# SwiGLU products of the prompt rows by one level of Strassen's scheme, with f and sums of w_down kept in DRAM between the gate/up and the down products

## The reference

```python
h = rmsnorm(x, g_pre_ffn)          # (1024 + 64, 1024)
gu = h @ w_gu                      # w_gu (1024, 2 * 2816)
gate, up = gu[..., :D_FF], gu[..., D_FF:]
f = (jax.nn.silu(gate) * up) @ w_down   # w_down (2816, 1024)
x = x + rmsnorm(f, g_post_ffn)
```

## Time and profile before

| | us |
|---|---|
| median of 3 runs (lowest, highest) | 1645.95 (1645.14, 1646.17) |
| span of the profiled execution | 1641.7 |
| around the span, to the median | 4.25 |
| PE busy | 1556.9 (95%) |
| DVE, ACT, POOL busy | 614.3, 410.7, 384.7 |
| output projection starts | about 721 |
| feed-forward part, from the first unit's matmul to the end | about 833 to 1641.7 |

### The profile page before, as it was taken

How to read it: one execution, slowest core, us unless ns; L and a number is a source line. 1 busy time by engine, 2 the same in 40 slices (tenths; PEclk the granted TensorE clock), 3 DMA queues, 4 the chain that set the end, 5 groups by cost and what they waited for, 6 DMA issues and landing times.

```text
span 1641.7 us, 23152 instructions
## 1 busy us (share of the span) xinstructions
PE 1556.9 (95%) x9350; PEld 1343.4 (82%) x9350; DVE 614.3 (37%) x983; ACT 410.7 (25%) x730; POOL 384.7 (23%) x459
## 2 busy tenths in 40 slices
PE   7999999998888889989999999999999999999994
PEld 6788888878655557768899999999999999999983
DVE  2334110106866545424532233332323333332355
ACT  4301121212254434433332121111112111111121
POOL 3254300013422212004462121211212121111111
PEclk9999999999999999999999999999999999999997
DMA  6323434129354029934356354544535354453434
GB/s 216 112 81 128 128 128 164 48 76 318 111 197 136 14 118 419 409 123 135 101 164 187 121 154 113 154 134 140 160 108 161 110 156 138 131 161 108 133 119 168
DMA packets 120290, 245.59 MB, mean 150 GB/s; under 512 B 20652, under 2 KB 82364, under 8 KB 115045
## 3 DMA queue, kind: packets, MB, share of 16 engines
q1 hardware_dynamic: 111400, 157.15, 29.8%
q0 software_dynamic: 6976, 71.32, 14.1%
q10 hardware_dynamic: 1824, 15.83, 2.3%
HBM read 214.08 MB, written 106.21 MB: 195 GB/s over the span
## 4 chain that ended last, share of the span: by engine, by line
PE 48%; POOL 3%; issue 2%; DVE 2%; ACT 0%; POOLq 0%; ACTq 0%; DVEq 0%
PE y_ps L2198 32%; PE x_ps L2212 8%; PE m_ps L2212 4%; PE d_ps L2212 4%; POOL xm L1671 1%; POOL h_lo L1683 1%; PE y_ps L1801 1%; DVE y L1766 1%; DVE acc L2129 0%; DVE acc L2133 0%; POOL stat L1664 0%; POOL stat L1673 0%; POOL stat L2008 0%; DVE acc L2117 0%; DVE m_lo L1740 0%
## 5 line engine op out<-in xcount | busy, mean ns | idle before, releaser
L2198 PE MATMUL y_ps<-h_hi,gu_hi 128*128 128x384 f32 (+1 forms) x1056 | 345.9, 328 | 0.0
L2198 PE MATMUL y_ps<-h_hi,gu_lo 128*128 128x384 f32 (+1 forms) x1056 | 345.5, 327 | 0.0
L2198 PE MATMUL y_ps<-h_lo,gu_hi 128*128 128x384 f32 (+1 forms) x1056 | 345.5, 327 | 0.0
L1976 POOL TENSOR_TENSOR f<-silu,f 128x384 fp32r<-128x384 f32 (+1 forms) x66 | 60.4, 915 | 605.0 <-ACT f L2038 417.8
L2198 PEld LDWEIGHTS y_ps<-h_lo,gu_hi 128*128 128x128 f32 x1056 | 198.3, 188 | 2.0
L2198 PEld LDWEIGHTS y_ps<-h_hi,gu_hi 128*128 128x128 f32 x1056 | 198.2, 188 | 2.0
L2198 PEld LDWEIGHTS y_ps<-h_hi,gu_lo 128*128 128x128 f32 x1056 | 198.2, 188 | 0.0
L514 PE MATMUL z_ps<-w_hi,h_hi 128*128 128x512 f32 x488 | 191.2, 392 | 4.3 <-POOL h_lo L342 4.3
L514 PE MATMUL z_ps<-w_lo,h_hi 128*128 128x512 f32 x488 | 190.4, 390 | 0.0
L2109 DVE TENSOR_TENSOR silu<-silu,y_ps 128x384 f32<-128x384 f32 (+1 forms) x66 | 35.1, 531 | 362.5 <-ACT silu L2035 357.0
L514 PE MATMUL z_ps<-w_hi,h_lo 128*128 128x512 f32 x432 | 168.8, 391 | 0.0
(11 more groups left out here) (266 smaller groups left out, 2218.2 us busy)
## 6 DMA issues: line engine op xcount, KB each, us to landing
ks_sample<-cache_k_win POOLq DMA_DIRECT2D x60, 544.0 KB, 6.0
vs_sample<-cache_v_win POOLq DMA_DIRECT2D x60, 544.0 KB, 7.4
raw<-w_gu SPq DMA_DIRECT2D x84, 256.0 KB, 6.5
K<-cache_k_win SPq DMA_DIRECT2D x8, 2048.0 KB
w_raw<-w_in SPq DMA_DIRECT2D x14, 1024.0 KB
z_scratch<-z_out SPq DMA_DIRECT2D x56, 256.0 KB, 2.0
raw<-w_down SPq DMA_DIRECT2D x22, 512.0 KB, 5.3
zr<-z_scratch SPq DMA_DIRECT2D x8, 1024.0 KB, 10.3
```

The lines of the kernel that those rows point to most:

```text
L1976: low = pool.tensor_tensor(f_lo[cut], f_t[:, 0:n_p], f_hi[cut].bitcast(F32), ALU.subtract)
L2198: mm = pe.matmul(bank[u % 2][:, 0:n], w[s][:, k, h, :], x[:, k, c:c + n], start=(k, m) == (0, 0), stop=(k, m) == (KT - 1, 2))
```

## The change

**Gate and up.** Group 0 is as before. For groups 1 to 10, rows 0 to 383 and 384 to 767, the two halves of K and the two halves of 128 columns make a 2x2 by 2x2 product, done with seven products instead of eight (Winograd's form). `chain(g, hh)` does it for gate (hh 0) and up (hh 1): products P1, P6, P7, P4 add up in one bank, P2, P5, P3 in another; ACT copies the first bank's state at three moments (`hold`), and DVE adds it to the second bank. The last 320 rows are multiplied as before, in between. The sums of rows (s1 to s4) are made once, by DVE and POOL; differences of weights (t2, t3, t4) are made by POOL for each chain. All weight blocks (128x512, hi and lo) go through a ring of eight slots, split six slots ahead.

**Down.** The down products of the prompt rows no longer stand between the units. After each group f and four sums of its parts, and four differences of w_down's parts, are stored to DRAM (`f_d`, `wt_d`). After the last group seven products follow, P1, P2, P6, P7, P5, P4, P3, each over 11 groups. A step is one group of one product: four tiles of 128 rows, three matmuls each. For it SP loads a block of f and one of w_down's (256 KB each) into a ring of four (`load_step`). The operands of the last product, P3, are loaded and split during P5 and P4 into buffers of their own (`load_last`). Sample rows are multiplied inside each gate chain.

**The rest.** The 120 window copies are issued four instructions at a time: eight in each of ten groups, then eight in each of the first five down products. The loop over groups is written out. The two fold matmuls are gone. Retention is wrapped in a scope that clears its semaphores and ends with one more barrier.

Core of the diff (`...` marks what is left out):

```diff
-                def step(g, par):
-                    first = 0
-                    for u in range(UNITS):
...
-                        unit(g, u)
-                        if not known(g, 0) and DOWN_AFTER[u]:
...
-                            down(g, par, first, DOWN_AFTER[u])
+                def product(n, bank, x, fresh):
+
+                    x_hi, x_lo = x
+                    cols = x_hi.shape[2]
+                    for k in range(HK):
+                        w_hi, w_lo = (s[n % RING][:, 128 * k:128 * k + 128] for s in (slot_hi, slot_lo))
+                        for m, (w, v) in enumerate(((w_hi, x_hi), (w_hi, x_lo), (w_lo, x_hi))):
+                            mm = pe.matmul(bank[:, 0:cols], w, v[:, k, :], start=fresh and (k, m) == (0, 0),
...
+                def chain(g, hh):
...
+                    product(n[0], chain_a, moving[P1], True)
+                    product(n[0], rest_ps[0], first_rows[0, 2], True)
...
+                    product(n[1], chain_b, moving[P2], True)
+                    product(n[1], rest_ps[0], first_rows[1, 2], False)
...
+                    product(n[2], chain_a, moving[P6], False)
...
+                    product(n[3], rest_ps[1], first_rows[0, 2], True)
+                    if not hh:
+                        sample_products(g - 1)
...
+                    product(n[4], chain_a, moving[P7], False)
...
+                    product(n[5], chain_b, moving[P5], True)
...
+                    product(n[6], chain_a, moving[P4], False)
...
+                    product(n[7], rest_ps[1], first_rows[1, 2], False)
...
+                    product(n[7], chain_b, moving[P3], False)
...
+                def step(s):
+                    p, g = divmod(s, GROUPS)
+                    n = Count.step(s)
+                    pe.wait_ge(lo_ready, n + 2)
+                    banks = pair_b if p in (P2, P5) else pair_a
+                    for i in range(4):
...
                 out.tensor(pe)
...
+                for g in range(1, GROUPS):
+                    chain(g, 0)
+                    chain(g, 1)
+                for s in range(STEPS):
+                    if s == Count.SUMMED_AT:
+                        sample_products(LAST)
+                    step(s)
+                for i in range(4):
+                    last_product(i)
```

SP's loads, of which the range of steps is 8 to 65 (P5 begins at step 44):

```diff
+                def load_step(s):
+                    if s < 4:
+                        sp.wait_ge(lo_ready, gate_up(LAST, s // 2, 7) + 1)
+                    else:
+                        sp.wait_ge(lo_ready, Count.step(s - 4) + 2)
+                    load_operands(s // GROUPS, s % GROUPS, raw_step[s % 4], step_landed[s % 4])
+
+                def load_last(g):
+                    if g >= 2:
+                        sp.wait_ge(last_lo_ready, 2 * g - 2)
...
+                for s in range(8, STEPS):
+                    load_step(s)
+                    if s >= GROUPS * P5 and (s - GROUPS * P5) % 2 == 0:
+                        load_last((s - GROUPS * P5) // 2)
```

ACT and DVE in a down step, and POOL behind the last group:

```diff
+                for s in range(STEPS):
...
+                    split_ahead(Count.step(s) + LEAD)
+                    split_ahead(Count.step(s) + 1 + LEAD)
+                    if s >= GROUPS * P5:
+                        split_last(s - GROUPS * P5)
...
+                    low_ahead(Count.step(s) + LEAD)
+                    low_ahead(Count.step(s) + 1 + LEAD)
+                    if s >= GROUPS * P5:
+                        low_last(s - GROUPS * P5)
+                    if s == 9:
...
+                        finish(0)
...
+                sums_of_f(LAST)
+                differences_of_down(LAST)
                 pool.wait_ge(half_set, 2)
...
+                root(0)
+                for p in range(5):
+                    pool.wait_ge(done, stepped(GROUPS * p))
+                    copies(40 + 4 * p, 42 + 4 * p)
+                    pool.wait_ge(done, stepped(GROUPS * p + 5))
+                    copies(42 + 4 * p, 44 + 4 * p)
```

1057 lines of the change are left out of this document (732 added, 325 removed).

## The result

The changed kernel takes **1912.64 us** (median of 4 runs, 1906.72 to 1918.47) against 1646.06 of the kernel before (4 runs): ratio 1.163, 95% interval 1.160 to 1.166. It is 16% slower. The forecast was 1622, the range 1593 to 1655. The matmuls that the change was to remove are gone (8974 in the profile where there were 9350); some 353 us of waits (1911.4 − 1641.7 + 83.3) came in their place, where the forecast had 60.

The account below looks back on a forecast made before the run. The prediction took PE's matmul count and spacing as the bound. From span 1641.7, −71.6 − 7.7 − 4.0 + 1.5 + 1.3 + 2.0 + 14.7 + 33 + 7.2 = −23.6 gave 1618.1, plus 4.25 for the runs' median: 1622, range 1593 to 1655.

Parts of the forecast that it names:

- POOL's 71.32 MB in 14.1%, 308 GB/s.: Copy rate from POOL's queue, used to price loads and copies in P1, P2, P6 and P7: 136.3 us, +14.7.
- DRAM traffic decides: Rival: in the down products all queues together fall below 269 GB/s, so the change is slower; 1661 at 250; chance 0.13.
- Inside a chain I add nothing.: Gate and up chains: no added wait, 45.5 us a group; six slots of lead cover a late split.
- chains stall: Rival: each of 20 gate and up chains waits 2 us for a late block, 40 us, giving 1662; chance 0.05.
- Matmuls: Gate, up and down: 240 matmuls of 384 columns and 132 down matmuls go, together −71.6 us.
- Last group's stall, sample products: End of last group: wait for POOL's split of sample rows, slow clock and fold matmuls' stretch go, −7.7 us.
- Tail: After the last matmul: 13.4 us remain to the end of the span, −4.0 us.
- Retention's scope: Retention's boundary: an added clear and barrier cost +1.5 us, bounds 0 and 3.4.
- Joints: Group 0 to the first chain +1.3 us; chains to the down part +2.0 us, bounds 0 to 5.
- The loop on SP: P5 and P4: P3's loads wait for DVE's split, two steps take 9.6 us where PE needs 5.45; +33 us.
- Copies in the down products: Down products: loads beside copies in P1, P2, P6, P7 cost +14.7 us, P5's first four copies +7.2.
- Copies come first: Rival: copies issued in a burst are served whole before loads, PE stalls 5 to 10 us more, 1630; chance 0.13.

Follow-up runs that it names:

- experiment 2: Changed kernel with w_down's differences, stores and next block load moved ahead of the group's other work for groups 2 to 10, all copies kept: 1741.38 us.
- experiment 13: Changed kernel with each window copy taking 272 rows of one sequence instead of 34 rows of each of eight: 1653.24 us.
- experiment 11: Changed kernel with w_down's block early, P3's loads behind two steps' loads, and no window copies: 1588.36 us.
- experiment 9: Changed kernel with w_down's block early and the down products' 40 copies moved to the input projection, P3's loads at their old place: 1638.58 us.

## Why the prediction was wrong

**The step that failed** is the price of the copies, in two places of the sum.

*"POOL's 71.32 MB in 14.1%, 308 GB/s."* That rate divides bytes by the time that packets took. Where copies stand one behind the other it was 126, and 127 over all sixteen. The row of the copies' own landing stood on the page that the prediction had before it: 7.4 us for a pair of 544 KB each, 1.11 MB, which is 151 GB/s. With 150 in place of 308 the first four down products would have been 25.2/321 + 17.8/150 = 197 us against 121.6, +76 instead of +14.7, and the forecast 1683: slower. The rival "DRAM traffic decides" named a turning point of 269 GB/s for all queues together and gave it 0.13; over the first sixteen copies all queues together moved 170. Its mechanism, that the amount read and written is the limit, isn't what ran: with the copies along one sequence all queues together moved 348 GB/s over the same sixteen. Addresses, piece size and copies in the queue decide it together. Nor is the limit of DRAM per core that the prediction cited the one that binds there: with the copies counted twice, read and written, it would be 248 GB/s more than those 348.

*"Inside a chain I add nothing."* The cover that was named, six slots of lead, lies behind the load, not ahead of it. The prediction looked at what each engine has to do (ACT 12 us a group, right) and not at when SP may ask for w_down's block: behind four stores that wait for POOL's differences, which stand behind four copies. With 36 us from one landing to the next issue and 46.4 for a group, a landing of up to some 10 us is covered; 5.3 and 7.0 cost nothing, 28.4 costs 18. The rival "chains stall" priced this as 2 us in each of 20 chains, with 0.05; it was 17 us in each of ten groups, 174 in all. Either remedy alone takes it away, to within 3 or 4 us of the 463 without copies: the order (experiment 2) or the addresses (experiment 13).

**Point by point.**
- *Matmuls:* right. 46.4 us a group without the stall, against 45.5; PE waits 0.85 us for DVE's sum in each group, 8.5 in all, and that is the difference.
- *Last group's stall, sample products:* right; neither the wait nor the fold matmuls are there.
- *Tail:* right. The last matmul starts at 1897.84 and ends at 1898.2, 13.2 us before the end; 13.4 was forecast.
- *Retention's scope:* taken as 1.5. POOL's idle time at that boundary is 3.45 us instead of 2.84, so 0.6. The whole retention block, between POOL's first instructions in it and behind it, takes 82.8 us instead of 78.7; over all the traces it is 81.1 to 83.2 in versions of the change and 78.7 to 80.4 in versions of the kernel before. So 1.5 was not too much, and where the rest arises was not taken apart.
- *Joints:* too low. The waits that the traces show there are given below, for experiment 11.
- *The loop on SP:* right in mechanism and nearly in size: 10.2 for 9.6 us a pair of steps, 41 us instead of 33.
- *Copies in the down products:* 14.7 + 7.2 = 21.9 us were forecast. With copies along one sequence, at 248 to 289 GB/s, somewhat below the 308 assumed, experiment 13 takes 299 us from the last cast to the end against 276 without copies: 23. So that sum was about right for the rate that it assumed; with the old addresses, at 127 GB/s, it is 110.
- *"Copies come first":* the mechanism was right (SP's queue gets 7 to 10% beside a burst) and its size wrong, 5 to 10 us instead of most of the 110. Its argument against, turns between queues, fell: turns are taken, but by pieces of very different size.
- *The clock:* taken as 0 since PE does not set the pace. In the loop this fits: from 1520 to 1582 us of experiment 9 the granted clock is 0.83, and PE still waits 1.1 to 5.9 us for DVE's split between its bursts. In the chains stalls of 13 to 19 us are followed by slow matmuls: twelve in 3.85 us (1348.80 to 1352.65) instead of 2.08, with a granted clock of 0.50 (1.2 GHz) from 1349 to 1352. There it adds 1.8 us a group, as PE's timeline shows:

```profile
1348.80 0.66 PE L2658 MATMUL y_ps<-h_hi,slot_hi 128*128 128x384 f32 x1 [17.25 <-DVE f L2471]
...
1352.65 0.31 PE L2658 MATMUL y_ps<-h_hi,slot_hi 128*128 128x320 f32 x1
```

With all stalls taken out the span is 1588.6 (experiment 11); the forecast for that case (1641.7 − 83.3 + 4.8) was 1563. 9 of the 25 us between are the chains' 0.9 a group. Most of the rest is waits of PE that the trace of experiment 11 shows: 3.85 us for DVE's split inside group 0, and 7.73 at the first chain (3.15 in the changed kernel), with 1.8 of slow matmuls behind it. There DVE makes f only behind a split that takes 3.75 us and the lo parts of the sums of h. The forecast had 1.3 for this joint. In the down part three waits for splits take 4.9 us, against 2.0 for the second joint.

The bounds of the terms, each at its end, add up to 1590 and 1652 and not to 1592 and 1651 as the prediction says; nothing hangs on it.

## What to carry to other kernels

A rate for a transfer is read from its issue-to-landing row at the load that it will have, not from the share of its queue; and a transfer that takes large pieces from rows megabytes apart is first tried along one stretch, which here was worth 259 us with no other edit, or in small rows (171 us). For each load that a change adds, write down when its queue may issue it, through every wait and store ahead of it there and on the engines that feed them, and how long a landing that covers: idle engines prove nothing about it. Background copies belong where the DMA engines are idle, a few at a time.

## What the runs showed of the hardware

- Copies from DRAM to DRAM over eight stretches 4 MB apart, in pieces of 34 KB and with several in the queue, move 126 GB/s and hold the DMA engines to 93%; along one stretch, with pieces of the same size, 289 at 87% (over all sixteen copies 127 and 248). Issued two at a time, the same copies from eight stretches moved 308 GB/s by packet time; six at a time, 173.
- How long a load lands beside copies depends on the size of the copies' pieces and on their addresses: a block of 1 MB took 28.4 us beside pieces of 34 KB, 14.7 beside rows of 2 KB, 7.0 beside pieces of 34 KB along one sequence, 5.3 without copies.
- DVE's split of 128x512 takes 0.69 us with POOL idle. In the chains, where POOL adds, the median for w_gu's blocks is 1.77 and the longest 4.0; the rows of the changed kernel by shape show the two means, in the chains (POOL busy) and in the down products (POOL idle):

```profile
L2460 DVE TENSOR_TENSOR slot_lo<-raw,slot_hi 128x512 fp32r<-128x512 f32 x104 | 142.2, 1385 | 41.3 <-ACT slot_hi L2289 41.3
...
L2460 DVE TENSOR_TENSOR slot_lo<-raw_step,slot_hi 128x512 fp32r<-128x512 f32 x132 | 88.4, 712 | 234.6 <-ACT slot_hi L2289 234.4
```

The 14 us of DVE's splits that the prediction counted in a group are so some 27 (142.2 us here, and 94.9 and 34.3 for the differences' and w_down's blocks, over ten groups). The Trainium skill ("SBUF — State Buffer", section "SBUF: two separate sides") describes a pair of ports that the two engines share and that one of them holds for a whole instruction; the two means agree. Inside the chains, where w_down's block comes in time, PE waits for nothing of DVE's but the 0.85 us a group named above, so it cost PE at most that there.
